# Layers with 1024 inputs in seven half-size products instead of eight, over three token parts instead of two

## What is computed

```python
a = rmsnorm(x, g_mix)
u = a @ w_in                      # 1024 -> 3080: q, k, v, two gate rows, o, B, C, h
h, C, n, m = mlstm_chunkwise(...) # 4 heads, chunks of the prompt, states of the sample
h_m = sigmoid(o) * (headnorm(h) * g_mh)
y_c = B * causal_conv3(C * h)
x = x + concat([h_m, y_c]) @ w_out          # 1024 -> 1024
f = rmsnorm(x, g_ffn)
x = x + (silu(f @ w_gate) * (f @ w_up)) @ w_down   # 1024 -> 2816 -> 1024
e = rmsnorm(p @ w_ple, g_ple)               # 256 -> 1024
x = x + sigmoid(x @ w_pg) * e               # 1024 -> 1024
y = rmsnorm(x, g_final)
```

## Time and profile before

| | |
|---|---|
| median of 3 runs | 2775.99 us (2769.67 to 2776.66) |
| span of the profiled execution | 2763.6 us |
| TensorE busy | 2677.8 us, 97% |
| VectorE, ScalarE, GpSimd busy | 703.5, 751.8, 795.7 us (25%, 27%, 29%) |
| mean granted TensorE clock | 0.983 |

### The profile page before, as it was taken

The page is one execution under the profiler, slowest core; times in us unless marked ns, Lnnn a source line. Parts: engine busy times, 40 slices in busy tenths (PEclk is TensorE's granted clock), DMA queues, the critical chain, the costliest instruction groups (busy, mean ns, idle before and its releaser), DMA issues.

```text
span 2763.6 us, 37564 instructions
## 1 busy us (share of the span) xinstructions
PE 2677.8 (97%) x14623; PEld 2409.6 (87%) x14623; DVE 703.5 (25%) x1296; ACT 751.8 (27%) x1355; POOL 795.7 (29%) x633
## 2 busy tenths in 40 slices
PE   7999999999999999999899999969999999999998
PEld 5788878788888888878799999969999999999998
DVE  5112241311111122233620323304111111113153
ACT  5332332412121211123443233214121212111143
POOL 2223344222222222222244333422222222232222
PEclk8999999999999999999999999989999999999999
DMA  6421131111111111113121112371111111111111
GB/s 184 128 52 38 38 114 46 46 46 46 46 51 47 46 46 46 46 54 108 39 84 54 38 38 66 92 39 47 46 47 46 47 46 47 46 46 46 46 50 74
DMA packets 251139, 159.87 MB, mean 58 GB/s; under 512 B 32945, under 2 KB 242129, under 8 KB 250641
## 3 DMA queue, kind: packets, MB, share of 16 engines
q1 hardware_dynamic: 241664, 153.91, 20.4%
q10 hardware_dynamic: 9360, 4.33, 0.5%
HBM read 139.95 MB, written 18.27 MB: 57 GB/s over the span
## 4 chain that ended last, share of the span: by engine, by line
PE 90%; issue 3%; SPq 2%; DVE 2%; POOL 1%; ACT 1%; DMA 1%; POOLq 0%; DVEq 0%; ACTq 0%
PE bank L553 28%; PE bank L556 28%; PE bank L557 28%; SPq L340 2%; POOL wlo L1820 1%; PE bank L585 1%; PE bank L674 1%; DVE AL L1597 1%; PE bank L608 1%; PE bank L607 1%; PE bank L654 0%; DMA wraw<-w_ple 0%; DVE AL L1694 0%; PE bank L612 0%; PE bank L723 0%
## 5 line engine op out<-in xcount | busy, mean ns | idle before, releaser
L553 PE MATMUL bank<-AH,whi 128*128 128x352 f32 (+1 forms) x3400 | 1206.3, 355 | 19.6 <-DVE wide L1638 5.0
L556 PE MATMUL bank<-AL,whi 128*128 128x352 f32 (+1 forms) x3400 | 1196.3, 352 | 0.0
L557 PE MATMUL bank<-AH,wlo 128*128 128x352 f32 (+1 forms) x3400 | 1195.2, 352 | 0.0
L1820 POOL TENSOR_TENSOR wlo<-wraw,whi 128x1024 fp32r<-128x1024 f32 x218 | 530.2, 2432 | 1509.8 <-ACT whi L947 1509.4
L553 PEld LDWEIGHTS bank<-AH,whi 128*128 128x128 f32 x3400 | 642.8, 189 | 90.4 <-issue 12.8
L556 PEld LDWEIGHTS bank<-AL,whi 128*128 128x128 f32 x3400 | 643.2, 189 | 59.4
L557 PEld LDWEIGHTS bank<-AH,wlo 128*128 128x128 f32 x3400 | 642.0, 189 | 60.1
L947 ACT ACTIVATE whi<-wraw 128x1024 fp32r<-128x1024 f32 x218 | 230.0, 1055 | 522.2 <-PE bank L553 480.4
L553 PE MATMUL bank<-hid,whi 128*128 128x352 f32 (+1 forms) x960 | 338.8, 353 | 30.8 <-POOL wlo L1820 25.5
L556 PE MATMUL bank<-hid,whi 128*128 128x352 f32 (+1 forms) x960 | 337.1, 351 | 0.0
L557 PE MATMUL bank<-hid,wlo 128*128 128x352 f32 (+1 forms) x960 | 336.8, 351 | 0.0
(11 more groups left out here) (220 smaller groups left out, 1485.8 us busy)
## 6 DMA issues: line engine op xcount, KB each, us to landing
wraw<-w_in SPq DMA_DIRECT2D x50, 512.0 KB, 3.9
wraw<-w_gate SPq DMA_DIRECT2D x44, 512.0 KB, 3.8
wraw<-w_up SPq DMA_DIRECT2D x44, 512.0 KB, 3.8
wraw<-w_down SPq DMA_DIRECT2D x44, 512.0 KB, 3.4
wraw<-w_out SPq DMA_DIRECT2D x16, 512.0 KB, 4.1
wraw<-w_pg SPq DMA_DIRECT2D x16, 512.0 KB, 4.0
next_x<-stored_x SPq DMA_DIRECT2D x1, 4224.0 KB, 13.2
wide<-stored_x SPq DMA_DIRECT2D x2, 2112.0 KB, 9.5
```

The lines of the kernel that those rows point to most:

```text
L553: first = nc.tensor.matmul(o, hi[:, k, cols_], mh, start=k == 0, stop=False)
L556: nc.tensor.matmul(o, hi[:, k, cols_], ml, start=False, stop=False)
L557: last = nc.tensor.matmul(o, lo[:, k, cols_], mh, start=False, stop=k == kc - 1)
L1820: nc.gpsimd.tensor_tensor(wlo[p][:, :], wraw[p][:, :], whi[p][:, :], ALU.subtract).then_inc(lo_done, 1)
```

## The change

**Blocks and products.** Every layer with 1024 inputs (`w_in` but for its gate rows, `w_out`, `w_gate`, `w_up`, `w_pg`) is worked in pairs of 128 output columns. A pair of outputs, the inputs in two halves of 512, and the tokens in two blocks make a 2x2 by 2x2 block product, which is now worked in seven products of half size instead of eight, in Winograd's form of Strassen's scheme. A product is 12 matmuls (4 steps of 128 inputs, three halves each). Its seven weight operands are `A11`, `A12`, `A22` and four sums `S1` to `S4`; its seven token operands are four blocks or their differences and three more sums (planes 0 to 6 of `qhi` and `qlo`). The other layers (`w_down`, `w_ple`, the gate rows) stay as plain products.

**Tokens** are in three parts of 704, 704 and 672, each in two blocks of 352, 352 and 336. Every weight is brought in, summed, rounded and subtracted once in each part. Raw pieces are of 1 MB (256 output columns), in two buffers; they are cut into entries of 128x512, seven for a pair, in a ring of five (`RING`), made four ahead of TensorE (`AHEAD`). The four sums of a pair are made by DVE in float32, five entries ahead.

**Results.** P1 and P2 share a bank, P6, P7 and P4 another one, P5 and P3 a third one; so P7 needs the bank that P6 filled, and P4 the one that P7 filled. ACT copies P1 to `t1`; DVE adds P6 (`u2`), P7 (`u3`), P5, P4 and P3 to it, and adds or multiplies the result into its target in a further instruction where the layer asks for that. The first pair of `w_out`, `w_gate` and `w_pg` has five banks and another order.

**Moved.** The token operands of a layer are made as whole halves of the inputs (128x1408): norm or merge, difference, rounding by ACT, subtraction by DVE (one of the seven by POOL). Merging heads, the sums of squares for the norms and q, k, v out of PSUM are DVE's work now, they were POOL's and ACT's. The gate rows' steps and the chunks' steps stand at fixed products among the pairs. The 16 small outputs and the 4 of the sample's states are no longer issued together. Nothing is a loop any more.

The diff replaces nearly the whole file. Its core, in order: the tables and sizes; the matmuls of a pair; on VectorE the sums of a pair's weights, P6, P7 and P5 out of PSUM, the token operands of `w_out` (128x1408 each); on GpSimd the low half of an entry:

```diff
+PRODUCTS = ("P1", "P6", "P5", "P7", "P2", "P4", "P3")
+WEIGHT_OF = {"P1": "A11", "P2": "A12", "P3": "S4", "P4": "A22", "P5": "S1", "P6": "S2", "P7": "S3"}
+RING = 5
+AHEAD = 4
+TW = 704
...
-                for k in range(kc):
-                    mh, ml = src[0][:, k, b0:b0 + bl], src[1][:, k, b0:b0 + bl]
-                    first = nc.tensor.matmul(o, hi[:, k, cols_], mh, start=k == 0, stop=False)
-                    nc.tensor.matmul(o, hi[:, k, cols_], ml, start=False, stop=False)
-                    last = nc.tensor.matmul(o, lo[:, k, cols_], mh, start=False, stop=k == kc - 1)
+                home = {"P1": a, "P2": a, "P5": b, "P3": b, "P6": c, "P7": c, "P4": c}
+                for j, name in enumerate(order):
+                    entry_ready(e)
+                    take(bk)
+                    for k in range(4):
+                        last = three(o, hi[:, k, :], lo[:, k, :], qhi[:, op, k, 0:q.N], qlo[:, op, k, 0:q.N],
+                                     name in begins and k == 0, k == 3)
+                    multiplied((q.n, st, i, name), bk, last)
+                    after(base + j)
...
...
+                        nc.vector.tensor_tensor(s1[:, :, :], v["A21"], v["A22"], add).then_inc(sums, 1)
+                        nc.vector.tensor_tensor(s2[:, :, :], s1[:, :, :], v["A11"], sub).then_inc(sums, 1)
+                        nc.vector.tensor_tensor(v["A21"], v["A11"], v["A21"], sub).then_inc(sums, 1)
+                        nc.vector.tensor_tensor(v["A11"], v["A12"], s2[:, :, :], sub).then_inc(sums, 1)
...
+                    if name == "P6":
+                        nc.vector.tensor_tensor(w2, t, c, add).then_inc(fc, 1)
+                    if name == "P7":
+                        nc.vector.tensor_tensor(w3, w2 if first else t, d, add).then_inc(fd, 1)
+                        corner(1, 1)
+                        released["u3"] = corner_out(target(1, 1), t if first else w3, w3, fb, b, "P5")
...
+                    nc.vector.tensor_tensor(t2_, b22, t1_, sub).then_inc(src_ready, 1)
+                    nc.vector.tensor_tensor(qraw[:, 6, :, 0:q.N], t2_, b11, sub).then_inc(src_ready, 1)
+                    nc.vector.tensor_tensor(qraw[:, 3, :, 0:q.N], b21, t2_, sub).then_inc(src_ready, 1)
+                nc.vector.tensor_tensor(qlo[:, i, :, 0:q.N], source(q, st, i), qhi[:, i, :, 0:q.N], sub).then_inc(low, 1)
...
+                nc.gpsimd.tensor_tensor(wlo[e % RING][:, :].rearrange(v, k=k), w.src, whi[e % RING][:, :].rearrange(v, k=k),
+                                        ALU.subtract).then_inc(lo_done, 1)
```

More of the change, by code:

```diff
@@ new lines, in __init__ @@
+        self.T = TW - TS if self.sample else TW
+        self.N = self.T // 2
+        self.TP = self.T - TS if self.sample else self.T
+        self.row0 = TW * n
+        self.tiles = [(t * P, min(P, self.T - t * P)) for t in range(NTILE)]
+        self.nch = NTILE - 1 if self.sample else NTILE
+        self.blocks = [slice(b * self.N, (b + 1) * self.N) for b in range(2)]
+        self.events = {}
+        base = 0
+        if self.sample:
+            self.events.update({1: ("scores", 5), 4: ("outputs", 5), 7: ("transposes", 5), 8: ("states", 0), 9: ("states", 1)})
+            base = 10
@@ new lines, in __init__, with event, down_before @@
+        for c in range(self.nch):
+            for kind, m in (("scores", 1), ("outputs", 4), ("transposes", 7)):
+                self.events[base + 8 * c + m] = (kind, c)
+        self.chunks = [c for m, (kind, c) in sorted(self.events.items()) if kind == "scores"]
+    def event(self, m, kind):
+        got = self.events.get(m)
+        return got[1] if got and got[0] == kind else None
+def down_before(p):
+    return p // 2 - 1 if p % 2 == 0 and 2 <= p < FFP - 1 else None
+class Entry:
+    def __init__(self, raw, src, total=0, first=False):
+        self.raw, self.src, self.total, self.first = raw, src, total, first
@@ L176, in keep @@
         return t
+    t1 = [keep(f"t1_{p}", [P, NW_]) for p in range(2)]
+    u2, u3 = keep("u2", [P, NW_]), keep("u3", [P, NW_])
     ident = keep("ident", [P, P])
@@ new lines, in pair, with nothing, last_operand, after @@
+            def pair(after, base):
+                for j in range(7):
+                    ahead()
+                    after(base + j)
+            def nothing(s):
+                return None
+            def last_operand(q, st):
+                def after(j):
+                    if j == (4 if st == "ffn" else 3):
+                        low_of(q, st)
+                return after
+            def pg_after(q):
+                def after(s):
+                    if s == 3:
+                        low_of(q, "pg")
+                    if q.n < 2 and s == 16:
+                        roots_of_x(supers[q.n + 1])
+                return after
```

3346 lines of the change are left out of this document (1735 added, 1611 removed).

## The result

The changed kernel takes 2943.9 us (2938.9 to 2947.7); the ratio to the kernel before is 1.0616 (1.0598 to 1.0633). It is slower by 6.2%. The forecast was 2819 us and slower by 1.6%: the direction held, the size did not, and 2944 us lies above the range (2675 to 2905) as well. The runs were made on several chips, so they are compared by their ratio to the kernel before, run on the same chip: the forecast stands for 1.0155, and 1.0616 came, 128 us more.

The account below looks back on a forecast made before the run. The prediction took TensorE's matmul columns as the bound; 2220 + 274 + 121 + 35 + 15 + 22 = 2687 us, plus 120 for VectorE against GpSimd and 12.4 on top, gave 2819 us, 1.6% slower, range 2675 to 2905.

Parts of the forecast that it names:

- short matmuls and clock: TensorE's short matmuls (recurrence, gates, norms, transposes) and lower-clock stretches: 203 us carried as 205, with some 8 for more clock falls.
- turns: VectorE and GpSimd wait out each other's SBUF steps, delaying TensorE: 120 us, bounded by 0 and some 230.
- small outputs: The 16 small outputs in SP's queue, mostly covered by products: 7 us of waits instead of 25.5.
- Matmuls: TensorE's large matmuls, costing by their columns: 2220 us, 235 us less than before.
- Start: Preparing the first product's token operands from all six tiles of the part: 48 us instead of 36.
- VectorE between the layers: At layer handovers TensorE waits for VectorE's steps that make the token operands: 121 us of waits.
- Chunks: At the recurrence's 18 chunks, VectorE's steps ahead of the transposes take 4.5 us against 1.9: 35 us.
- Gate rows: Scans and weights stand between banks that TensorE wants back: about 5 us a part, 15 us.
- the engines hardly meet: Rival: GpSimd takes its turns while VectorE waits for products; 2699 us, faster by 2.8%, chance 0.27.
- all hidden: Rival: VectorE's stretches between layers are hidden as well; 2578 us, chance 0.08.
- both are the bound in the feed-forward layer: Rival: GpSimd and VectorE, 26.4 of 26.6 us per w_gate and w_up pair, leave no slack; 2909 us, chance 0.13.
- The floor: Rival: matmuls stop getting cheaper at 352 columns; 34 us more, 2853 us, within the forecast's width, no separate chance.

Follow-up runs that it names:

- experiment 2: Changed kernel with GpSimd's low half of each weight entry cut to 2 of 128 output columns (pool_tiny): 1.0012 of the kernel before.
- tiny_no_small: Changed kernel with GpSimd's low halves of weights cut to 2 of 128 columns and the 16 small outputs left out: 0.9905 of the kernel before.
- pool_tiny: Changed kernel with GpSimd's low half of each weight entry cut to 2 of 128 output columns: 1.0012 of the kernel before.
- pool_split: Changed kernel with GpSimd's low halves in shorter steps, two per weight entry and four for the tokens, same arithmetic: 1.0498 of the kernel before.
- split4_fill: Changed kernel with GpSimd's low halves of weights in four steps of 128x128, plus short filler matmuls between layers and in the feed-forward layer: 1.0737 of the kernel before.
- fill_more: Changed kernel with 4002 short unused matmuls ahead of TensorE's waits at 119 places: 1.0501 of the kernel before.
- pool_quarter: Changed kernel with GpSimd making only a quarter of each weight entry's low half: 1.0132 of the kernel before.
- small_spread: Changed kernel with the 16 small outputs spread behind every second raw piece of the third part's feed-forward layer: 1.0662 of the kernel before.

## Why the prediction was wrong

**The step that failed is the term "short matmuls and clock".** The trace after, cut at the first and the last large matmul, gives each term of the sum its measured size:

| us of span | forecast | measured |
|---|---|---|
| large matmuls, nominal | 2220 | 2220 |
| ahead of the first, behind the last one | 48 + 21 | 44 + 20 |
| TensorE's waits between them | 313 | 327 |
| short matmuls and clock | 205 | 335 |
| span | 2807 | 2946 |

The waits are the 121, 35, 15 and 22 us of the sum and the 120 of turns. They came out 14 us above the forecast; nearly all that was missing, 130 of 139 us, is in the last term. It holds 159 us that large matmuls took beyond nominal, where 39 were there before and 8 more were taken for the clock, and 177 us of short matmuls, where 156 were there before and 8 more were taken.

**By the runs.** Three runs divide the 0.0461 (128 us) that were missing in time: turns 0.0604 where 0.0432 (120 us) was taken, 48 us; small outputs, from 1.0012 to 0.9905, 0.0107 where 7 us were taken, 23 us; the rest, 0.9905 where 0.970 was taken, 57 us, of which fillers give back 22. The slow products are in the first and the last of these: the 48 us are the 47 that go with the turns' waits (experiment 2), and in tiny_no_small the waits between the first and the last large matmul are 174 us, where the sum without turns and small outputs has 186, while short and slow matmuls take 284 where it has 205.

*Matmuls, 2220 us:* right in count (14220) and at 352 columns; at 336 the columns' rule is 9 us short.

*Start, 48 us:* the first product began at 43.5. Right, a little high.

*VectorE between the layers, 121 us and 50 for turns:* the waits there sum to 163 us (in to out 47, out to feed-forward 55, feed-forward to `w_pg` 29, `w_pg` into the next part 32). As waits this is the forecast. But the forecast took the waits as the chain less products at full speed, and part of the products ran at the lower clock; the chain was therefore longer than forecast by what the slow products hid. One place is in the trace, VectorE and GpSimd in the second part's handover:

```profile
1276.28 3.69 DVE L1304 TENSOR_TENSOR s<-s,wraw 128x512 f32<-128x512 f32 x1
```

```profile
1274.83 4.60 POOL L2041 TENSOR_TENSOR qlo<-wide,qhi 128x1408 fp32r<-128x1408 f32 x1
```

GpSimd's one low half of the tokens takes 4.6 us there, and a sum of 0.69 us behind it 3.69. The prediction priced the turns by GpSimd's steps of 1.25 us alone and left this longest one out.

*Turns, 120 us:* 168 us in time, of which 114 are waits: as waits, which is how the term was worked out, the size held, and so did the mechanism. The upper bound doesn't follow from its own figures: 120 and 3 us in each of 30 cycles are 210, not 230. The division was off too: in the feed-forward layer 24 waits of 0.64 and 0.84 us ahead of P7's bank make 17 us (27 were forecast), in `w_pg`'s later pairs 23 us stand where 31 were forecast; more of the price lies between the layers and around the first pairs, as pool_tiny shows part by part (waits and slow products together, the changed kernel and then pool_tiny): `w_out` from 24.7 to 12.1 us in the first part, `w_ple` with the first four pairs of the feed-forward layer from 33.4 to 15.3. The Trainium skill's rule (SBUF — State Buffer, Who interferes with whom) is that one engine waits for the whole of the other's instruction. By that rule, the runs agree: shorter steps gained 33 us (pool_split), and the sum above took 3.69 us beside a step of 4.60. That short steps have a price of their own, split4_fill showed.

*Short matmuls and clock, 205 us with 8 for the clock:* this step failed. I had read the clock off two stretches behind waits and multiplied it with hardly anything, while forecasting some hundred waits. Of the 120 us that large matmuls took more beyond nominal than before, 75 lie in stretches at the lower clock and some 30 at the waits' edges, a cost at the full clock that the sum didn't have at all. What fillers could get back is less, 32 us (fill_more), since VectorE's chains take the place of the rest. The short matmuls took 21 us more than before, 8 were forecast; why, no run has taken apart.

*Chunks, 35 us:* the 18 waits ahead of the heads' transposes, which this term priced, sum to 34.3 us. By its own figures (4.5 us in six cases of ten, 3.5 in the others, against 1.9) it should have been 40. All waits in the eight pairs of the chunks are 14.0, 15.6 and 31.9 us in the three parts, 61 us: 27 us more, 19 of them in the third part, which has the sample's steps as well and of which the prediction had only a share of 9 us. Which of the steps it is, no run has taken apart.

*Gate rows, 15 us:* 17 us of waits in `w_in`'s fourth pair. Right.

*Small outputs, 7 us:* 32 us of waits, and 30 to 34 in time by the runs; wrong by reading the 25.5 us of the earlier trace rows as one wait of the queue, with products as cover. The transfers stop more than the weights: they cost the same spread out among other work.

So the waits' total came near in part by luck: small outputs and chunks were short by 25 us each, the feed-forward layer, `w_pg` and the handovers too dear by 10, 8 and 8, and for the 21 us of norms' squares and odds hardly 9 are left.

**The rivals.** That the engines hardly meet is refuted by pool_quarter and pool_tiny, and with it "all hidden". That both are the bound in the feed-forward layer (2909 us) came nearest in time and is wrong as a mechanism: that layer has the smallest waits of all, with TensorE busy for 49.36 of 50 us in its windows. The floor is not there at 352 columns, and at 336 it is 1.8 ns. No rival was about the clock, so no bound of the range held it: a term taken at 8 us came out at 120.

## What to carry over

A stage that prepares operands on VectorE and GpSimd together pays, in every stretch where TensorE has nothing else to do, for VectorE's steps and for GpSimd's steps that they wait out; count the longest step of either engine first, since the other waits for all of it. Moving the work onto one engine is no way out by itself: in VectorE's own queue it cost the same here. When a change turns a full TensorE into one with a hundred waits of over a microsecond, price what comes behind the waits as a term of its own (here 120 us for 283 us of added waits), and remember that where a chain on another engine sets the end, winning the clock back wins little. Saved columns are sure only as far as the work that saves them lies beside products and not between two layers.

## What the hardware showed that I had not expected

- While the 16 small outputs ran, mostly as packets of 4 bytes, all engines came to a stop. Between two matmuls of one product, with no semaphore between them in the code, TensorE stood for 4.6 us, and in small_spread VectorE stood 4.9 us in the middle of the feed-forward layer's adds. The profile names no releaser in the core ("issue", "remote"). That the engines' instructions come through the same full DMA engines would fit: of the changed kernel's 209 packets of the kind "instruction" one, at 2280.4 us, took 10.3 us, where the next longest took 1.6 and the median is 0.95. But no run tested it, and it stays open; the kernel before, mostly loops, loses the same 34 us to the outputs.
- GpSimd took 0.35 us for a subtraction of 128x8, 0.58 to 0.61 for 128x128 and 0.92 for 128x256 beside VectorE, so splitting the steps of 128x512 once paid (33 us), and twice, tried with fillers only, cost more than it gave.
- A wait costs TensorE some 0.24 us more than its idle time, at the full clock as well: 0.16 us in the last large matmul ahead of it and 0.08 in the first one behind. At 570 us, a wait of 0.64 us puts 1.20 us between two starts with one matmul between them, where 0.32 would be nominal. Over the changed kernel this is some 30 us more than before, and no term had it.
